# Neighbourhood attention on one core: the scores of both units of a group issued together, ahead of the products with the values

## What is computed

```python
s_loc = einsum('bhrjqd,bhrjkd->bhrjqk', qb, kg) + bias; s_loc = where(valid, s_loc, -inf)
s_ctx = einsum('bhrjqd,bhkd->bhrjqk', qb, k_ctx)
p = softmax(concatenate([s_loc, s_ctx], -1))
o = einsum(p[..., :nk], vg) + einsum(p[..., nk:], v_ctx)
```

## Time and profile before

| | us |
|---|---|
| median of the runs (3523.0 to 3524.93) | 3524.09 |
| the profiled execution, its own time | 3527.01 |
| span of its trace | 3525.1 |
| attention stage, from the first scores to the last OL | 2108.9 to 2454.5 |
| TensorE busy over the span | 3450.4 (98%) |

### The profile page before, as it was taken

The page is one execution under the profiler, slowest core; times in us unless marked ns, Lnnn a source line. Parts: engine busy times, 40 slices in busy tenths (PEclk is TensorE's granted clock), DMA queues, the critical chain, the costliest instruction groups (busy, mean ns, idle before and its releaser), DMA issues. The chain is left out here.

```text
span 3525.1 us, 47182 instructions
## 1 busy us (share of the span) xinstructions
PE 3450.4 (98%) x19104; PEld 3009.0 (85%) x19104; DVE 1503.0 (43%) x2605; ACT 1038.7 (29%) x1566; POOL 1240.4 (35%) x819
## 2 busy tenths in 40 slices
PE   8999999999999999999999999999999999999997
PEld 8988887888888888888888879999888888888886
DVE  6855535656244444443531117886241112111116
ACT  5521211335211111111352316776261111111113
POOL 6411117436322222222451306665352222222223
PEclk9999999999999999999999999999999999999998
DMA  4533327651222222222163547785101111111111
GB/s 176 193 117 116 125 87 262 200 191 60 71 67 72 66 66 72 72 72 78 54 223 142 183 154 188 194 195 146 59 31 42 37 42 36 36 42 36 42 36 66
DMA packets 173815, 365.92 MB, mean 104 GB/s; under 512 B 16968, under 2 KB 98440, under 8 KB 171945
## 3 DMA queue, kind: packets, MB, share of 16 engines
q1 hardware_dynamic: 168168, 352.55, 31.4%
q10 hardware_dynamic: 5440, 10.49, 0.9%
HBM read 285.38 MB, written 77.59 MB: 103 GB/s over the span
## 5 line engine op out<-in xcount | busy, mean ns | idle before, releaser
L148 POOL TENSOR_TENSOR w_lo<-w_raw,w_hi 128x1024 fp32r<-128x1024 f32 x207 | 501.9, 2425 | 1395.6 <-ACT w_hi L142 1395.4
L156 PE MATMUL ps_front<-a_hi,w_hi 128*128 128x512 f32 (+1 forms) x1584 | 568.5, 359 | 5.5 <-DVE y_prod_c L1151 2.6
L156 PE MATMUL ps_front<-a_lo,w_hi 128*128 128x512 f32 (+1 forms) x1584 | 566.6, 358 | 0.0
L156 PE MATMUL ps_front<-a_hi,w_lo 128*128 128x512 f32 (+1 forms) x1584 | 566.1, 357 | 0.0
L142 ACT ACTIVATE w_hi<-w_raw 128x1024 fp32r<-128x1024 f32 x207 | 217.4, 1050 | 719.0 <-PE ps_front L156 375.6
L156 PE MATMUL ps_r<-a_hi,w_hi 128*128 128x512 f32 (+1 forms) x1056 | 374.9, 355 | 1.1 <-POOL a_lo L2061 0.9
L156 PE MATMUL ps_r<-a_lo,w_hi 128*128 128x512 f32 (+1 forms) x1056 | 374.0, 354 | 0.0
L156 PE MATMUL ps_r<-a_hi,w_lo 128*128 128x512 f32 (+1 forms) x1056 | 373.5, 354 | 0.0
L156 PEld LDWEIGHTS ps_front<-a_hi,w_hi 128*128 128x128 f32 x1584 | 299.8, 189 | 52.6 <-POOL a_lo L2061 3.1
L156 PEld LDWEIGHTS ps_front<-a_lo,w_hi 128*128 128x128 f32 x1584 | 299.8, 189 | 43.9 <-issue 0.7
L156 PEld LDWEIGHTS ps_front<-a_hi,w_lo 128*128 128x128 f32 x1584 | 299.4, 189 | 43.7
(11 more groups left out here) (310 smaller groups left out, 7238.7 us busy)
## 6 DMA issues: line engine op xcount, KB each, us to landing
w_raw<-in_w_all SPq DMA_DIRECT2D x205, 512.0 KB, 3.5
ada_w_l<-in_ada_t SPq DMA_DIRECT2D x59, 512.0 KB, 3.5
v_hl<-v_d SPq DMA_DIRECT2D x128, 128.0 KB, 3.1
t_tail_f<-in_ada_t SPq DMA_DIRECT2D x24, 512.0 KB, 4.1
spec<-gout_f SPq DMA_DIRECT2D x80, 128.0 KB, 2.2
g_spec_c<-spec ACTq DMA_DIRECT2D x20, 512.0 KB, 5.0
v_d<-z_v_l SPq DMA_DIRECT2D x10, 1024.0 KB, 4.2
q_hl_l<-q_d SPq DMA_DIRECT2D x32, 320.0 KB, 7.3
```

Of the source, the lines that this page charges most:

```text
L148: pool.tensor_tensor(wl[:, s, 0:width], raw[:, s, 0:width], wh[:, s, 0:width].bitcast(F32), ALU.subtract).then_inc(w_split, 1)
L156: last = pe.matmul(out[:, c0:c1], w[:, c % 2, blk * 128:blk * 128 + 128], x[:, c0:c1], start=start and b == 0 and term == 0, stop=stop and ...
```

## The change

TensorE issues the scores of both units of the group two ahead, 2g+4 and 2g+5, one after the other behind the three turnings and ahead of M(g-1). Before, S(2g+3) stood between the two local turnings and S(2g+4) ahead of M(g-1). So every odd unit's scores move earlier by most of a step. ScalarE, GpSimd and VectorE get orders to match, and each prologue one unit more.

```diff
@@ TensorE
-                    for u in range(3):
+                    for u in range(4):
                         scores(0, u)
 ...
                     if turned and local(2 * g):
                         turn_local(i, 2 * g)
-                    if scored(g, last):
-                        scores(i, 2 * g + 3)
-                    if turned and local(2 * g):
                         turn_local(i, 2 * g + 1)
                     if turned:
                         turn_ctx(i, g)
                     if scored(g + 1, last):
                         scores(i, 2 * g + 4)
+                        scores(i, 2 * g + 5)
                     if g:
                         mix(i, g - 1)
@@ ScalarE (prologue: exps for 4 units)
                         high_local(i, 2 * g)
                         high_local(i, 2 * g + 1)
-                    if scored(g, last):
-                        exps(i, 2 * g + 3)
                     if turned:
                         high_ctx(i, g)
                     if scored(g + 1, last):
                         exps(i, 2 * g + 4)
+                        exps(i, 2 * g + 5)
                     if g:
                         out_high(i, g - 1)
@@ GpSimd (prologue: bias_mask(0, 5) too)
                     if scored(g, last):
                         norm(i, 2 * g + 2)
-                    if scored(g + 1, last):
-                        bias_mask(i, 2 * g + 5)
-                    if scored(g, last):
                         norm(i, 2 * g + 3)
                     if scored(g + 2, last):
                         bias_mask(i, 2 * g + 6)
+                        bias_mask(i, 2 * g + 7)
@@ VectorE (prologue: minima(0, 3) too)
                     if scored(g, last):
                         recip(i, 2 * g + 2)
+                        recip(i, 2 * g + 3)
+                    if turned and local(2 * g):
+                        low_local(i, 2 * g)
                     if g >= 2:
                         out_low(i, g - 2)
-                    if scored(g, last):
-                        minima(i, 2 * g + 3)
                     if turned and local(2 * g):
-                        low_local(i, 2 * g)
+                        low_local(i, 2 * g + 1)
                     if scored(g + 1, last):
                         minima(i, 2 * g + 4)
-                    if scored(g, last):
-                        recip(i, 2 * g + 3)
-                    if turned and local(2 * g):
-                        low_local(i, 2 * g + 1)
+                        minima(i, 2 * g + 5)
                     if turned:
                         low_ctx(i, g)
```

More of the change, by code:

```diff
@@ L2649, in prologue @@
                     bias_mask(0, 4)
+                    bias_mask(0, 5)
                 def step(i, g, last):
@@ L2706, in prologue @@
                     recip(0, 1)
+                    minima(0, 3)
                 def step(i, g, last):
```

## The result

The changed kernel takes 3556.51 us (median of 4 runs, 3556.21 to 3558.33) against 3524.51 of the kernel before, run on the same chip: 32 us slower, a ratio of 1.0085 with a 95% interval of 1.0074 to 1.0097. Its profiled execution took 3556.2 us, 29.2 more than the 3527.0 of before. 3543.3 was forecast, 19.2 us above before; the direction and the place are right, the size is 10 us short by the profiled executions and 13 by the medians.

A forecast was written before the change was run, and what follows sets the result against it. TensorE was taken as the bound, busy 42.14 of 43 us. Halves cost 8 x 1.32 + 7 x 1.10 = 18.3 us, ends 0.9: 19.2 us over the median 3524.1 gave 3543.3 us, range 3527 to 3559.

The forecast's parts named there:

- The wait for N: TensorE's TL of odd units waits 0.43 us for norms, 15 times; gone for good, at most 9 us to win.
- TensorE's own work of 20.09 us per half: Sum of TensorE's start-to-start times over a half's five steps; the half's length if nothing waited, against 20.58 us before.
- TensorE stays the bound: Rival: TensorE sets the pace and the old wait is simply gone; 3517 us, or 3515 at most gain; chance 5%.
- The loop through HL, LL, OL, LL, Mi, E, E, OH: Chain over ScalarE and VectorE from one HL to the next, without TensorE work; 4.57 us, against 2.94 before.
- TC for LC: New TensorE wait in each half, as LC stands behind both Mi on VectorE; about 0.6 us.
- M for OL: New TensorE waits in each half, as OL stands behind HL and LL; about 0.3 us and, one step on, 0.8.
- E waits far less for Mi: Sign of the forecast on ScalarE: its waits for VectorE's Mi fall far below those of before; no size given.
- The queues overlap less with both Mi and both E together: Rival: instructions on the ScalarE and VectorE queues overlap less than the rows show; 3554 to 3565 us, chance 12%.
- A half over two pairs: Half spanning two pairs of heads, OL(9) not between the two LL; 1.10 us more than now, against 1.32 inside one.
- The start: Stage's beginning, before S(10): any win or loss swallowed by TensorE's 5.00 us wait for keys at 2134.19.
- The clock: Rival: new waits of up to 0.9 us drop TensorE to 1.2 GHz, 3.1 us each half; 3590 us, chance 2%.
- The rule on the pipe: Skill's rule for VectorE, set aside: no operation starts until the pipe is empty; loop 4.8 us, time 3550.

The follow-up runs named there:

- e9: e7 with OL(9) of a pair moved from the end of VectorE's step 10 to step 1 of the next pair; 3520.9 us, ratio 0.9986 to the kernel before.
- e4: The changed kernel with OH and OL of the second head on partitions 0 to 63 instead of 64 to 127 (output wrong); 3547.0 us, ratio 1.0061.
- e3: The changed kernel with OL(g-2) one place earlier on VectorE, ahead of LL(2g); 3530.0 us, ratio 1.0011 to the kernel before.
- e11: The changed kernel with OH and OL of both heads on partitions 64 to 127 (output wrong); 3569.6 us, ratio 1.0124 to the kernel before.
- e1: The kernel before with only TensorE's new order, the other engines keeping theirs; 3553.7 us, ratio 1.0076.
- e7: The kernel before with TensorE's new order and VectorE's Mi(2g+3), R(2g+2), OL, LL, LL, R(2g+3), Mi(2g+4), LC; 3529.7 us, ratio 1.0013.
- e8: The kernel before with only OL(g-2) moved behind LL(2g) on VectorE; 3570.5 us in one run.
- e5: The kernel before with OH and OL of the second head on partitions 0 to 63 (output wrong); 3525.9 us, ratio 1.0004.

## Why the prediction was right, and where it was short

- **The wait for N goes.** Right: one of 0.4 us is left in the stage, at its start. (Of the 15 waits before, the one at 2272.55 was 0.78 us and not 0.43; without it a half is 20.55, not 20.58.)
- **TensorE's own work of 20.09 us per half.** Right to 1%: e9, without waits, shows 20.2. The forecast's rival "TensorE stays the bound" needed orders that leave no chain, and e9 is that kernel.
- **The loop through HL, LL, OL, LL, Mi, E, E, OH.** Right in every link, and its two outlets, TC for LC and M for OL, are the waits that took the place of the old one. In first heads' steps the loop is 4.53 us (HL 2324.37 to 2328.90), 4.57 forecast (its eight terms, as written, add up to 4.58). TC's wait was 0.51 and 0.86 us (0.6 forecast), M's in step 2 0.94 to 1.06 (0.8). M's wait in step 1 (0.3) came at 0.2 us in the halves inside a pair: M starts 0.92 us behind the S ahead of it (2329.51 and 2330.43) in place of 0.70, and 0.55 behind OL (2329.88). Over two pairs it didn't come (2307.51 and 2308.21), since OL(9) starts at 2307.16.
- **A sign that was wrong.** "E waits far less for Mi" stands among the signs. E's waits for Mi rose from 52.4 to 102.5 us. The forecast's own loop has E behind Mi as a link, so that wait had to be there.
- **The size.** 19.2 us were forecast; 29.2 came by the profiled executions, 32.0 by the medians. The step that failed is the list of the loop's terms, "LL(2g) to OL(g-2): 0.46", "OL to LL(2g+1): 0.35", "E(2g+5) to OH(g-1): 0.83" and "OH to the next HL: 0.26". They were read from one head's rows and taken for all; for the second head they are 0.59, 0.46, 0.93 and 0.41. e4, with the second head's rows on the first's partitions, has a stage of 363.4 us, 16.9 above before; the 19.2 of the forecast was too high for that kernel by 2.3 (mostly in the first half of the first pair, counted with 1.32, which is no longer in e4 than before), and the partitions make 12.5 us of the 29.4 (9.5 by the medians).
- **What of the hit is luck.** The time lies 2.5 us inside the upper end of the range, and between the 3554 and 3565 of the rival "The queues overlap less with both Mi and both E together". Overlap was lost, but not for that reason: in the first heads' steps, which have both Mi and both E together, Mi starts 0.47 us behind LL (2325.68 and 2326.15) and E 0.83 behind E (2327.00 and 2327.83), as forecast, and e3 leaves them together and comes within 4 us of before. The range's upper part was put there for less overlap in every loop; it was lost in one head's, for a cause that the prediction doesn't name.
- **A half over two pairs is cheaper** (21.68 against 21.90). In the changed kernel it is the longer one, 22.67 against 22.27, for it holds the second head's OH and OL in its loops. That is the same failed step again, and not the reasoning on OL(9). In e4, where the partitions don't count, the halves over two pairs and inside one are 21.59 and 21.86 us, and OH(9) to the Mi of the next step is 1.79 us (2299.90 to 2301.69) in place of 2.07 in the changed kernel (2306.75 to 2308.82). So the forecast's way through a half holds within 0.1 us once the four terms are right. M's waits in e4, from half to half:

```profile
2284.38 0.35 PE L2547 MATMUL ps_o<-pt_hi,v_hl 128*128 128x256 f32 x1 [0.63 <-DVE a_lo L2694]
...
2305.97 0.36 PE L2547 MATMUL ps_o<-pt_hi,v_hl 128*128 128x256 f32 x1 [0.62 <-DVE a_lo L2694]
...
2327.83 0.36 PE L2547 MATMUL ps_o<-pt_hi,v_hl 128*128 128x256 f32 x1 [0.63 <-DVE a_lo L2694]
```

- **The start** was swallowed by the wait for keys: TensorE waits until 2133.35 after, 4.08 us, in place of 2134.19 and 5.00; the granted clock of the first 44 us is 0.84 in both. Right.
- **The clock.** Waits of up to 1.06 us and ten transposes in a row left it at 2.4 GHz in all steady stretches (granted clock 1.00). The rule of the Trainium skill that spoke for a fall ("TensorE: Matmul & The Clock Gate", section "Part 4: PE-mode transpose") brought nothing here.
- **The rule on the pipe.** LC, Mi and R start 0.07 to 0.09 us before the end of the operation ahead of them, in both kernels. The sentence that the prediction took from the Trainium skill's "VectorE: DVE Perf Modes", section "The DRAIN you can't avoid", doesn't fit these rows. But the prediction left out that the same paragraph says that an instruction which is not held starts earlier, and sends the reader to another section of that page, "Two Vector instructions with no wait between them". This says that an instruction whose operands start in another quadrant of partitions than those ahead of it starts only when all earlier ones are finished. VectorE's rows of e4, the change and e11 agree with it: 0.48, then 0.59. It gives no price, and is on VectorE alone; but it would have sent the author to the rows of the second head, which have one: in the kernel before, OH at 2292.95 and HL at 2293.35 are 0.40 us apart.

Two of the experiments' own estimates each left out a wait of S for Mi: e1's in several kinds of step, e7's in the one step of a pair that differs from the others.

## What to carry to other kernels

When several in-order queues are reordered together, write down the chain from each operation to itself one step later across all engines; an operation that merely drains a buffer, put behind two that wait, can cost more (44 us in e8, one execution) than the wait that the reordering removes (9 us at most). Do it for every kind of step, the short ones and the seams between loops above all, since the engine that sets the pace there need not be that of the full step. And take start-to-start times from rows of every variant of an operation: here the two heads differ only in their partitions.

## What the runs showed of the hardware that was not expected

- On VectorE, an operation on partitions 64 to 127 between operations that start at partition 0 loses its overlap on both sides: 0.59 and 0.46 us in place of 0.47 and 0.33 (the change, e11; gone in e4). It costs nothing where the queue has slack (e5).
- ScalarE does the same: E to OH 0.93 in place of 0.82 us, OH to HL 0.41 in place of 0.26 (the change; gone in e4, with 0.81 and 0.27).
- Behind a wait, TC takes 0.06 us longer to pass: TC to S is 0.41 us (2306.36, S at 2306.77), 0.35 without one. M takes hardly longer: 2.17 us behind a wait (2290.44, TL at 2292.61), 2.15 without one.
